# Index scores of two heads in the two halves of the array, without zero padding

## The reference, cut to what matters

```python
s_ix = jax.nn.relu(jnp.einsum('bqhd,bkd->bqhk', q_ix.astype(f32), k_ix) * (IDX_DIM ** -0.5))
score = jnp.einsum('bqh,bqhk->bqk', w_ix.astype(f32) * (N_IDX_HEADS ** -0.5), s_ix)
score = jnp.where(chunk_ok, score, -jnp.inf)
top_val, top_idx = lax.top_k(score, topk)
```

## Time and profile before

| | |
|---|---|
| median of 3 runs | 4192.29 us (4190.23 to 4199.5) |
| span of the profiled execution | 4196.1 us |
| PE busy, share of the span | 3800.4 us, 91% |
| PE weight loads | 2963.7 us, 71% |
| DVE busy | 2700.0 us, 64% |
| ACT busy | 1163.7 us, 28% |
| POOL busy | 56.1 us, 1% |
| mean granted TensorE clock | 0.951 of full speed |

### The profile page before, as it was taken

How to read it: one execution, slowest core, us unless ns; L and a number is a source line. 1 busy time by engine, 2 the same in 40 slices (tenths; PEclk the granted TensorE clock), 3 DMA queues, 4 the chain that set the end, 5 groups by cost and what they waited for, 6 DMA issues and landing times. The chain is left out here.

```text
span 4196.1 us, 53481 instructions
## 1 busy us (share of the span) xinstructions
PE 3800.4 (91%) x19261; PEld 2963.7 (71%) x19261; DVE 2700.0 (64%) x4918; ACT 1163.7 (28%) x2323; POOL 56.1 (1%) x176
## 2 busy tenths in 40 slices
PE   4999998889887999999969999889987789999995
PEld 2555555657655999999935555566665589999995
DVE  2289995774565666666636999668547556666665
ACT  2122223443553111111112222234336321111112
POOL 0000000000000000000000000000000000000000
PEclk7999999999888999999989999999999899999997
DMA  4121214201101111111011222421100011111111
GB/s 179 41 79 55 92 56 142 81 7 55 31 11 39 45 48 45 45 45 45 11 59 66 85 76 65 159 68 29 51 26 9 11 56 45 45 45 45 45 35 47
DMA packets 277298, 232.73 MB, mean 55 GB/s; under 512 B 30974, under 2 KB 254046, under 8 KB 275326
## 3 DMA queue, kind: packets, MB, share of 16 engines
q1 hardware_dynamic: 277118, 230.42, 17.3%
HBM read 170.03 MB, written 60.42 MB: 55 GB/s over the span
## 5 line engine op out<-in xcount | busy, mean ns | idle before, releaser
L1501 PE MATMUL psum<-h_split,gate_up_split 128*128 128x352 f32 x6336 | 1019.2, 322 | 43.9 <-DVE gate_up_split L1615 43.9
L1501 PEld LDWEIGHTS psum<-h_split,gate_up_split 128*128 128x128 f32 x6336 | 1011.2, 188 | 48.2 <-issue 47.1
L876 PE MATMUL psum<-arena 128*128 128x512 f32 (+4 forms) x2304 | 756.1, 486 | 0.0
L1645 DVE TENSOR_TENSOR arena<-arena,psum 128x352 f32<-128x352 f32 x1056 | 513.6, 521 | 318.2 <-PE psum L1501 318.2
L876 PEld LDWEIGHTS psum<-arena 128*128 128x128 f32 (+1 forms) x2304 | 413.0, 181 | 329.2 <-issue 290.8
L1501 PE MATMUL psum<-hid_split,down_split 128*128 128x352 f32 x3168 | 522.9, 325 | 11.1 <-DVE down_split L1615 11.1
L1501 PEld LDWEIGHTS psum<-hid_split,down_split 128*128 128x128 f32 x3168 | 516.4, 190 | 11.6 <-issue 11.6
L1194 PE MATMUL psum<-arena 128*128 128x512 f32 (+4 forms) x1040 | 413.7, 514 | 80.9 <-DMA arena<-q_by_map 45.9
L1212 PE MATMUL psum<-arena 128*128 128x64 f32 (+2 forms) x2432 | 337.9, 275 | 37.0 <-DVE arena L1280 20.2
L1212 PEld LDWEIGHTS psum<-arena 128*128 128x128 f32 (+2 forms) x2432 | 309.4, 194 | 72.3 <-ACT arena L1280 27.7
L1034 DVE MAX8 top<-arena 128x8 f32<-128x384 f32 (+6 forms) x394 | 346.6, 880 | 13.5
(11 more groups left out here) (142 smaller groups left out, 3139.5 us busy)
## 6 DMA issues: line engine op xcount, KB each, us to landing
gate_up_raw<-in_w_gate SPq DMA_DIRECT2D x44, 512.0 KB, 3.7
gate_up_raw<-in_w_up SPq DMA_DIRECT2D x44, 512.0 KB, 4.7
down_raw<-in_w_down SPq DMA_DIRECT2D x44, 512.0 KB, 3.5
arena<-in_w_in SPq DMA_DIRECT2D x24, 768.0 KB, 7.1
q_by_map<-arena SPq DMA_DIRECT2D x48, 256.0 KB, 2.3
arena<-q_by_map SPq DMA_DIRECT2D x48, 256.0 KB, 3.2
q_by_map<-arena SPq DMA_DIRECT2D x16, 512.0 KB, 3.5
arena<-bias_strips SPq DMA_DIRECT2D x4, 2048.0 KB, 10.4
```

Of the source, the lines that this page charges most:

```text
L876: ins = nc.tensor.matmul(m.ps[0:n, o + n0:o + n1], m.hT[:, c, c0:c0 + n], w[:, c, n0:n1], start=(c == 0), stop=(c == KC - 1))
L1501: ins = nc.tensor.matmul(out, w[i], x[k], start=(first and n == 0), stop=(last and n == 2))
L1645: nc.vector.tensor_tensor(x, x, bank(m, down_bank[p])[:, 0:PIECE], ALU.add).then_inc(s.added, 1)
```

## The change

The padded key goes. `kixT` keeps one key in both halves, in half of its space; the other half stays unused, so that what follows lies where it did. The memset on POOL, its semaphore and DVE's wait go. Each score matmul takes the 64 partitions of its own head, lower for even heads and upper for odd ones, queries and keys alike. The units are put in an order in which the two heads of a pair follow each other for the same keys, so that they go to banks 6 and 7. Only the first of a pair waits, and it waits for the Relu of all units before it. DVE's wait ahead of an add names the unit that last touched the same slice of the sum: the one just before for odd heads.

```diff
@@ place @@
-    m.kixT, e = at(e, 2, KEYS)
+    m.kixT, _ = at(e, KEYS)
+    e += 2 * KEYS
@@ stage_project_index @@
-             "cache_in", "next_in", "zeroed"]
+             "cache_in", "next_in"]
-        @block.gpsimd
-        def _(pool):
-            nc.gpsimd.memset(m.kixT[:, :, :], 0.0).then_inc(s.zeroed, 1)
-
                 for r in range(2):
-                    ins = nc.vector.tensor_copy(m.kixT[64 * r:64 * r + 64, r, kcol:kcol + n], t[64 * r:64 * r + 64, 4, 0:n])
+                    ins = nc.vector.tensor_copy(m.kixT[64 * r:64 * r + 64, kcol:kcol + n], t[64 * r:64 * r + 64, 4, 0:n])
                 ins.then_inc(s.kept, 1)
-            dve.wait_ge(s.zeroed, 1)
@@ stage_project_select @@
-            for h in range(NIX):
+            for h0 in range(0, NIX, 2):
                 for k0 in range(0, blk.keys, BANK):
-                    units[blk.n].append((n_units, h, k0, min(k0 + BANK, blk.keys)))
-                    n_units += 1
+                    for h in (h0, h0 + 1):
+                        units[blk.n].append((n_units, h, k0, min(k0 + BANK, blk.keys)))
+                        n_units += 1
@@ score, on PE @@
-                    if x >= 2:
-                        pe.wait_ge(s.relu_done, x - 1)
+                    if x >= 2 and h % 2 == 0:
+                        pe.wait_ge(s.relu_done, x)
+                    half = slice(64 * (h % 2), 64 * (h % 2) + 64)
                     nc.tensor.matmul(bank(m, 6 + x % 2)[0:blk.rows, 0:k1 - k0],
-                                     m.qixT[:, h // 2, blk.q0:blk.q0 + blk.rows],
-                                     m.kixT[:, h % 2, blk.key0 + k0:blk.key0 + k1], start=True, stop=True
+                                     m.qixT[half, h // 2, blk.q0:blk.q0 + blk.rows],
+                                     m.kixT[half, blk.key0 + k0:blk.key0 + k1], start=True, stop=True
                                      ).then_inc(s.scored, 1)
@@ the adds, on DVE @@
                     if h:
-                        dve.wait_ge(s.added, x - parts + 1)
+                        before = x - 1 if h % 2 else x - 2 * parts + 1
+                        dve.wait_ge(s.added, before + 1)
```

## The result

The changed kernel takes 4255.74 us (median; 4252.69 to 4259.84) against 4195.89 for the kernel before on the same chip: ratio 1.0144, 95% interval 1.0129 to 1.0158, 59.9 us longer. The sign was forecast, the size was not: the forecast was 8.8 us, the top of the range 4222. The profiled execution spans 4253.6 us, 57.5 more than that of before, and its mean granted clock is 0.936 of full against 0.951.

What follows compares the result with a forecast made beforehand. PE was taken to bound projection with selection, 14 us behind DVE's end. A layer's +3.4 after the gates and +1.0 before made +4.4, two layers +8.8: 4204.9 us from the profiled span, 4201 on the median; range 4190 to 4222.

Steps and rivals of the forecast that it cites:

- The chain through a pair: Score pairs on PE: streaming, tail, two Relus and resume set a 512-column cycle of 2.35 us, against 1.81 before.
- full overlap: Rival for score pairs: a pair streams in 2 s, only last pairs shrink; two layers +3.4 us, 4196; chance 0.12.
- the working for the four parts of blocks 6 and 7: Per-layer changes: block 7 second +1.60 and first +0.44, block 6 second +0.83 and first +0.40 us.
- three records' time for a pair: Score matmuls: a pair streams for 3 s, between 4 s without overlap and 2 s with full; forecast's chance 0.45.
- The switch: PE going from 128 to 64 contraction rows and back: could cost 0.16 us each time, taken as 0.
- the other side: Rival: 64-row score matmuls stream in half the time, s of 0.21, 512 cycle 1.93; 4178 us; chance 0.08.
- the prediction's price of that rule: If changing tiling mode drains PE, two tails for each of about seven parts: 2.2 us a layer, 4.4 in both.
- the prediction has +0.85: Block 2's first part: two longer cycles +0.86, last pair -0.32, wait for the previous block's last Relu 0.3 us.
- the clock: Rival: clock falls behind parts, up to 3.5 us a tile; +14 in two parts of each layer, 4215; chance 0.13.
- a clock that falls everywhere: Clock rival in all five parts after the gates of each layer: +35 us, 4236, left out of the range.
- the parts after the gates: Block 5's second part and both parts of blocks 6 and 7, summed to +3.4 us a layer.
- the signs that the prediction named against itself: Profile after: couples faster than 2.0 us, gaps between tiles and pairs, or new half-clock stretches following the parts.

Runs made afterwards that it cites:

- e1: The kernel before with the new order of units and the wait for both banks, still 128 zero-padded rows: 4232.78 us, 1.0087.
- e7: The changed kernel plus an unread 128-row matmul behind each pair that has another to follow: 4207.12 us, 1.0022 to the kernel before.
- e9: The changed kernel with every head on the lower 64 rows and each unit waiting for the Relu two units back: 4273.89 us, 1.0169 to the kernel before.
- e3: The changed kernel with one line changed, each unit waiting for the Relu two units back: 4227.64 us, 1.0077 to the kernel before.
- e5: The kernel before with only the new order of units and DVE's matching waits: 4197.98 us, 0.9998.
- e8: The changed kernel with pairs issued between the next tile's steps and a plan constant moved from 147 to 144: 4172.34 us, 0.9939 to the kernel before.
- e11: The kernel before (128 padded rows) with units issued between the next tile's steps and the plan constant at 144: 4186.25 us, 0.9963.
- e2: The changed kernel with the old order of units and the old wait, keeping the 64-row operands: 4247.64 us, 1.0116 to the kernel before.

## Why the prediction was right and wrong

**Right.** PE bounds the stage and DVE stays 14 us ahead. Busy time on the score line shrinks while its idle grows. The chain through a pair (stream, tail, Relu, Relu, resume) is the one that sets the cycle: 2.30 measured at full clock for a forecast 2.35, and 2.67 in e1 for 2.66. With full overlap put in, the working for the four parts of blocks 6 and 7 gives +1.7 us in a layer; in e7, where all four are at full clock, they take 1.7 more. The memset was taken as free; its removal was not tried by itself.

**The overlap was mis-sized.** The forecast took three records' time for a pair and argued that the second record of one head can't run beside the first of the other. A last pair takes 1.06, two records and a switch, so that argument was wrong: the rival "full overlap" (chance 0.12) is what the chip did. The 0.05 left in the 512 cycle, 2.30 against 2.35, can't tell the two, since Relu sets it in either case.

**The switch was put at nothing, and it costs.** A change of shape costs 0.2 us each way. For block 3's last pair that is 1.06 for 0.86 and, in the tile behind it, 10.64 for 10.54. The trace of the kernel before had shown it, and the prediction misread it: the six records of the earlier trace rows are four of 32 rows and, in the same line, two of 128 rows. Narrow windows of the kernel before part them:

```profile
442.67 0.38 PE L876 MATMUL psum<-arena 128*128 128x256 f32 x1
442.98 0.24 PE L891 MATMUL psum<-const_tile,arena 32*128 32x32 f32 x1
...
443.34 0.33 PE L891 MATMUL psum<-const_tile,arena 128*128 128x128 f32 x1
```

The 32-row records start 0.06 to 0.08 apart, not 0.10. The first of them starts 0.31 after a tile record of 256 columns, behind which the next record otherwise starts after 0.21. The first 128-row transpose starts 0.15 after the last of the 32-row ones and takes 0.33, where its like takes 0.27. The 0.09 before the first record is the same that stands before a pair of 64 rows. So a part of the price stood in the trace of the kernel before, in the very rows that were read against it. The rival "the other side" leans on the same reading; it fell by other evidence, the cycle of 2.30. The Trainium skill, TensorEngine Tiling (Array Packing), Key Properties, has a change of mode drain the engine, and on this the trace agrees with it against my reading. Full overlap at +3.4 and the prediction's price of that rule, +4.4, make +7.8, and e7 measured +9.3; that the two are close is in part luck, since e7's excess lies mostly in three groups of units that spend more time at half clock.

**Two groups of units are missing from the sum.** Block 3's second part is a last pair alone and should have stood there with -0.43. The sample block, which runs straight into block 2's first part, isn't priced at all: together they take 9.95 us in the kernel before, 12.51 in the changed kernel (all of it at half clock) and 13.80 in e1, where the prediction has +0.85.

**The step that failed was the clock.** The prediction left it out of its sum. It stood as a rival with a chance of 0.13, priced at up to 3.5 us per tile behind a part: +14 in two parts of each layer, +35 in five, and "a clock that falls everywhere" was left out of the range. The runs put about 50 of the 59.9 us down to it. Three things were wrong in the rival. It priced only the tiles (0.7 to 2.5 us more behind nine of a layer's twelve groups of units, 13.3 us a layer), while the pairs stretch as well, from a cycle of 2.30 to 3.25; that is about half of the 50 us. It counted only the parts after the gates, while block 4's second part falls for longer too: 13.7 us at half clock where the kernel before has the 6.9 of the earlier trace rows, and the tile behind takes 12.95 for 10.48. And it saw the cause in the idle time between pairs alone: the earlier trace rows shows the clock fall after PE sat still, and I weighed 1.28 of 2.35 streaming against 1.71 of 1.81. e1 has the waits with 128 rows and nearly keeps its clock; e9 has 128 rows' timing with 64 rows and loses it. The narrower matmuls were the other part of the cause, and they were the change itself.

The Trainium skill, TensorE: Matmul & The Clock Gate, Part 1, tells of a kernel that cycled through PSUM banks and whose short idles between groups of matmuls made the clock swing; the pair wait adds such idles, and 60.7 us at half clock in e3 become 84.8 in the changed kernel. With 128 rows the trace shows little of it: the same wait takes e5's 13.2 us to 16.7 in e1. On rows in use the profile of the kernel before said nothing, since all of its 512-column matmuls use 128; that should have widened the range upward, because a clock at 0.99 can fall but hardly rise.

**By its own marks.** Of the signs that the prediction named against itself one came true: new half-clock stretches follow the parts.

## What to carry to other kernels

When a change makes matmuls smaller in rows or puts waits between them, price the clock before the columns: here halving the score matmuls' streaming time won 10 to 14 us where other matmuls covered the waits (e8 against e11), and the lower clock took about 50. Two units that fill all the banks at once have lost their double buffering, so put other matmuls between such pairs first and then see on which engine the stage ends; zero padding that costs streaming time can still be the cheaper way to keep a tightly spaced stretch at full clock. And when a row of the profile counts several records, part them by shape before reading a spacing from it.

## What was not expected of the hardware

- Float32 matmuls of two row halves, two records each, overlap fully: a pair of 512 columns takes 1.06 us with the switch, where four records one behind the other take 1.71.
- Matmuls on 64 rows can let the granted clock fall to 1.2 GHz in a stretch where PE was busy 13.93 of 14 us (e9); the same timing with 128 rows ran at 1.00. In the whole stage it is 92 us at half clock against 13.
- Adding matmuls that nobody reads saved 48.6 us (e7).
- A change between 128-row and 64-row matmuls costs 0.2 us each way, and the part of it that stands before the first record, 0.09, is there between 128-row matmuls and 32-row transposes too.
- The same part of the same kernel ran at full clock in one layer and partly at half in the other (e2, block 7's second part: 7.41 and 10.73 us for sixteen records).
